# A hybrid encoder kernel in which the 64x64 matmuls change row halves, the sample is padded to 64 tokens and GpSimd makes part of the low weights

## The chip, the cores and the metric

The kernel runs on one core of a Trainium2 chip. The metric is the device time of one execution in microseconds. TensorE (PE) does the matmuls, VectorE (DVE), ScalarE (ACT) and GpSimd (POOL) the elementwise work, and SyncE (SP) issues the transfers.

## What is computed

Two layers of a streaming encoder trunk, for a prompt of 512 tokens and a sample of 32 tokens with states and caches of its own. In each layer (CHUNK = 64, head dimension 64, width 1024):

```
hn = rmsnorm(x);  proj = hn @ w_in          # retention q,k,v,g | GLA q,k,v,g,low | attention q,k,v
retention (4 heads): scores = (q k^T) * decay, intra = scores v, inter = q S * q_decay, S = gamma^L S + (k*k_decay)^T v
GLA (4 heads):  b = cumsum(log_f);  scores[t,s] = sum_d q[t,d] k[s,d] exp(b[t,d]-b[s,d]),  s <= t
                intra = scores v,  inter = (q exp(b)) S,  S = exp(b_last) S + (k exp(b_last-b))^T v
attention (8 heads): own chunk and 8 chunks back, learned relative bias, softmax
x = x + concat[norm(ret)*silu(g), norm(gla)*silu(g), att] @ w_out
x = x + relu(rmsnorm(x) @ w_up)^2 @ w_down
```

## The kernel before

**Units.** All weights are cut into units of 128 columns (1024x128 each, 512 KB). A layer has 28 units of the input projection, 8 of the output projection and 4 groups of 16 for the MLP, 100 in all. SP loads a unit into one of 4 buffers `raw` (`load`, L364), ACT rounds it to fp32r as `whi` (`split`, L487), VectorE takes the remainder `wlo = raw - whi` (`rest`, L762), and TensorE multiplies in three passes (hi by hi, hi by lo, lo by hi) with 544 tokens in two halves of 272 (`products`, L1245): 24 matmuls for a half unit, 48 for a unit. There are two buffers each of `whi` and `wlo`. `rest` of unit n+1 stands in VectorE's queue in unit n, `begin(n)` (L1236) has TensorE wait for it, and `load` has SP wait for it before it reuses the raw buffer.

**Slots.** The mixing of the tokens is cut into stages that are hung by hand into the half units (`PE_STEPS`, `DVE_STEPS`, `ACT_STEPS`). In slot (n, half) TensorE runs the stage and then the 24 products of that half (L1523). The stages in `MID` (L79) stand behind the first 12 products instead. VectorE and ACT have the reading side of the same stages in their queues, each in program order.

**The stages that matter here**, with two groups g of two heads; head p of a group lies in partitions 64p to 64p+63:
- diagonal (L1293), (5,0) for GLA and (11,1) for retention: q by k per chunk and head, 32 matmuls of 64x64 in the order of `chunks()` (p, then g, then chunk c), which read rows 64p and write rows 64 (c mod 2) of PSUM bank M0 + p, and 4 for the sample of 32 columns. VectorE multiplies them by a mask into `Pm` and `Ps` (L928).
- level 0 to 5 (L1309), (5,1) to (8,0): the scores of GLA at block sizes H = 32 to 1. ACT makes factors (`level_f`, L658), VectorE multiplies them into q (`level_q`, L881) and GpSimd into k (`level`, L444), TensorE does 32 matmuls 64x64 by 32 columns and from level 1 on 4 for the sample (64x32 by 16 columns), and VectorE copies the results into `Pm` and `Ps` under a mask (L953). On TensorE a level is done in two pieces: head 0 ahead of the 24 products, head 1 behind the first 12.
- tok (L1332): transposes of k and v; kv (L1350): the states, 32 matmuls in the order c, g, p, with rows 64 (c mod 2) and bank M0 + c mod 2, and 4 for the sample with 32 rows. VectorE runs a chain of 18 state updates (L989).
- out (L1369): 32 matmuls `Pm` by v, with rows and PSUM rows 64 (c mod 2), and 32 matmuls q by S, with rows 64p; out_s (L1387) the same for the sample: 4 of 32x32, 4 of 64x32.
- gn and back (L1405): the norm of the heads on VectorE and ACT, then transposes back; for retention in slot (15, 1), behind 12 products. `newton` (L774) is VectorE's part of the norm.

GpSimd has in a layer two clears, the k products of the levels, eight sums of squares after the output projection with one reduction over the partitions, and 32 additions in the MLP.

The order of the chunks, and what stands between the products:

```
def chunks(head=None):
    for p in range(2) if head is None else (head,):
        for g in range(2):
            for c in range(NC):
                yield p, g, c
...
products(n, (xhi, xlo), all_kc[:4], parts=(half,), last=False)
for st in PE_STEPS.get((n, half), []):
    if st[0] == "level" or st in MID:
        stage(st, 1)
products(n, (xhi, xlo), all_kc[4:], parts=(half,), first=False)
```

Of the kernel before, what the change touches and what calls it, by code (L numbers as in the profile page):

```python
# [20 lines left out]
P = 128  # L21
# [76 lines left out]
for _steps in (DVE_STEPS, ACT_STEPS):  # L98
    for _u in range(4):
        _slot = (15 + 3 * _u, 0)  # L100
        _steps[_slot] = _steps[_slot] + [("parts", _u, 0)]
SLOTS = [(n, half) for n in range(2, N_IN) for half in range(2)]
# [34 lines left out]
def hybrid_encoder(nc, x, wu, w_low, a2, small, wf, bias, bias_s, st_ret, st_gla, ck, cv,  # L137
# [3 lines left out]
    with ctx:  # L141
# [63 lines left out]
        Ps = at("Ps", [TS, 4, TS], o + 14336)  # L205
        S = at("S", [P, 2, NC + 1, HD], o + 14848)
        Ss = at("Ss", [P, 2, 2, HD], o + 19456)
        O = at("O", [P, 20 * HD], o + 20480)
        end1 = o + 25600
# [18 lines left out]
        PS = ctx.enter_context(nc.psum_tensor("PS", [P, 8, 512], F32))  # L228

# [5 lines left out]
        def sem(name):  # L235
# [21 lines left out]
            "pe_back", "back_read", "rot_ready", "ret_scaled", "o_cleared", "s_cleared",  # L257
# [101 lines left out]
        with nc.Fori(0, L) as layer:  # L359
            with nc.Block() as block:  # L360
                @block.sync
                def _(sp):

                    def load(n, j):  # L364
                        if not (isinstance(n, int) and n == RAW):
                            sp.wait_ge(sems["w_lo"], n - RAW)
                        sp.dma_start(raw[j][:, :], wu[layer * UNITS + n, :, :]).then_inc(sems[f"w_in{j}"], 16)
# [65 lines left out]
                def _(pool):  # L433
# [8 lines left out]
                    nc.gpsimd.memset(S[:, :, 0, :], 0.0).then_inc(sems["s_cleared"], 1)  # L442

# [14 lines left out]


# [19 lines left out]
                def _(act):  # L479
# [36 lines left out]
                    def stage(st):  # L516
# [32 lines left out]
                        elif what == "tok":  # L549
# [22 lines left out]
                        elif what == "out_s":  # L572
                            act.wait_ge(sems["o_cleared"], 1)
                            act.wait_ge(sems["pe_out_s"], st[1] + 1)
                            nc.scalar.activation(O[0:TS, 16 * HD:], PS[0:TS, M0, 0:256], ACT.Copy) \
# [11 lines left out]
                        elif what == "back":  # L587
                            kind = st[1]
                            act.wait_ge(sems["pe_back"], kind + 1)
                            for g in range(2):  # L590
                                j = 2 * (1 - kind) + g
                                nc.scalar.activation(oT[j][:, 0:TP], PS[:, M0 + g, :], ACT.Copy)
                                ins = nc.scalar.activation(oT[j][:, TP:T], PS[:, M0 + 2, g * TS:(g + 1) * TS], ACT.Copy)
# [160 lines left out]
                def _(dve):  # L754
# [137 lines left out]
                    def stage(st):  # L892
# [35 lines left out]
                        elif what == "diag":  # L928
# [4 lines left out]
                            dve.wait_ge(sems["pe_diag"], kind + 1)  # L933
                            for p in range(2):
# [5 lines left out]
                                    Ps[:, 2 * p:2 * p + 2, :], PS[0:TS, M0 + 2 + p, 0:2 * TS].rearrange("p (g c) -> p g c", g=2),  # L940
                                    dm_sb[0:TS, kind, 2 * p:2 * p + 2, 0:TS], ALU.mult)
# [11 lines left out]
                        elif what == "level":  # L953
# [17 lines left out]
                            for p in range(2):  # L971
# [5 lines left out]
                                if H <= TS // 2:  # L977
                                    out = Ps[:, 2 * p:2 * p + 2, :].rearrange("p s (b x h) -> p s b x h", x=2, h=H)[:, :, :, 1, :]
                                    m = lm_sb[0:TS, l:l + 1, 0:16].to_broadcast([TS, 2, 16]).rearrange("p s (b h) -> p s b h", h=H)
                                    ins = nc.vector.copy_predicated(out, m, PS[0:TS, M0 + b0 + p, 256:288]  # L980
                                                                    .rearrange("p (s b h) -> p s b h", s=2, h=H))
# [41 lines left out]
                        elif what == "out_s":  # L1023
                            kind = st[1]
                            dve.wait_ge(sems["outs_act"], kind + 1)
                            for p in range(2):
                                o_v = O[0:TS, 16 * HD:].rearrange("p (a b c) -> p a b c", b=2, c=HD)[:, :, p, :]
                                nc.vector.tensor_tensor(o_v, PS[0:TS, M0 + 1 + p, 0:2 * HD].rearrange("p (a c) -> p a c", c=HD),
# [108 lines left out]
                    for n, half in SLOTS:  # L1137
# [3 lines left out]
                        if half == 0 and rest_first:  # L1141
# [5 lines left out]
                        if half == 0 and not rest_first:  # L1147
# [72 lines left out]
                def _(pe):  # L1220
# [45 lines left out]
                    def stage(st, quarter=0):  # L1266
# [26 lines left out]
                        elif what == "diag":  # L1293
# [9 lines left out]
                            for p in range(2):  # L1303
                                for g in range(2):
                                    r, o = slice(64 * p, 64 * p + 64), slice(g * T + TP, (g + 1) * T)
                                    last = mm(PS[0:TS, M0 + 2 + p, g * TS:(g + 1) * TS], k[r, o], q[r, o])
                            last.then_inc(sems["pe_diag"], 1)
                            give((0, 1, 2, 3), "diag_read", kind + 1)
                        elif what == "level":  # L1309

                            l, piece = st[1], quarter % 2
# [11 lines left out]
                            if H <= TS // 2:  # L1323
                                for p in (piece,):
                                    for g in range(2):
                                        r, o = slice(64 * p, 64 * p + 64), slice(g * T + TP, (g + 1) * T)
# [459 lines left out]
```

## Time and profile before

| | us |
|---|---|
| median of 3 runs | 1461.77 (1461.52 to 1462.84) |
| profiled execution, from first to last instruction | 1460.0 |
| PE busy | 1418.2 (97%) |
| DVE busy | 799.6 (55%) |
| ACT busy | 532.5 (36%) |
| POOL busy | 147.8 (10%) |
| mean granted TensorE clock | 0.992 of full |

The page gives no total for the profiled execution other than its span; the runs' times stand 1.8 us above it, for what lies before the first and behind the last instruction. Layer 0 fills the span to about 724 us, layer 1 repeats it from 733 on; every time named below is one of layer 0, and layer 1 has the same 712.7 us later.

### The profile page before, as it was taken

How to read it: one execution, taken by the hardware profiler on the slowest of the kernel's cores; microseconds unless marked ns; L12 is line 12 of the kernel's file. 1: busy time of each engine (PE TensorE's matmuls, PEld its weight loads, DVE VectorE, ACT ScalarE, POOL GpSimd, SP SyncE). 2: the span in 40 equal slices, each digit the busy share in tenths (PEclk: the TensorE clock that was granted, in tenths of full speed). 3: DMA queues.
4: the chain of work that ended last, by engine and by line, in shares of the span. 5: the costliest groups of instructions: out<-in, count | busy, mean ns of one | idle time of the engine just before them, and what ended most of it. 6: DMA issues, size and time to landing. Idle time of an engine off the chain costs nothing. (4 is left out here: it accounts for less than half of the span.)

```text
span 1460.0 us, 30389 instructions
## 1 busy us (share of the span) xinstructions
PE 1418.2 (97%) x12680; PEld 1373.7 (94%) x12680; DVE 799.6 (55%) x1245; ACT 532.5 (36%) x892; POOL 147.8 (10%) x133
## 2 busy tenths in 40 slices
PE   7999999999999999999899999999999999999995
PEld 6999898899999999999889998989999999999995
DVE  4788766744534435344368967776453353443533
ACT  5332465743313223133153226656332231322322
POOL 0110000022020110200202000000201102002012
PEclk9999999999999999999989999999999999999998
DMA  5212343222222222222221133342222222222223
GB/s 193 74 45 65 100 149 93 74 87 88 87 88 86 87 87 88 90 90 89 64 76 48 60 97 106 92 122 73 85 90 87 87 86 86 86 86 87 88 87 107
DMA packets 60683, 129.98 MB, mean 89 GB/s; under 512 B 11984, under 2 KB 29648, under 8 KB 60592
## 3 DMA queue, kind: packets, MB, share of 16 engines
q1 hardware_dynamic: 60592, 128.69, 27.4%
q8 instruction: 66, 1.08, 0.3%
q14 instruction: 25, 0.20, 0.0%
HBM read 121.46 MB, written 7.21 MB: 88 GB/s over the span
## 5 line engine op out<-in xcount | busy, mean ns | idle before, releaser
L1234 PE MATMUL PS<-xhi,whi 128*128 128x272 f32 x1920 | 564.7, 294 | 10.9 <-issue 8.3
L1234 PE MATMUL PS<-xhi,wlo 128*128 128x272 f32 x1920 | 556.7, 290 | 0.0
L1234 PE MATMUL PS<-xlo,whi 128*128 128x272 f32 x1920 | 554.4, 289 | 0.0
L765 DVE TENSOR_TENSOR wlo<-raw,whi 128x1024 fp32r<-128x1024 f32 x200 | 252.7, 1264 | 378.9 <-ACT whi L495 378.2
L495 ACT ACTIVATE whi<-raw 128x1024 fp32r<-128x1024 f32 x200 | 211.6, 1059 | 605.3 <-PE PS L1234 605.0
L1234 PEld LDWEIGHTS PS<-xhi,whi 128*128 128x128 f32 x1920 | 363.3, 189 | 22.2 <-issue 17.8
L1234 PE MATMUL PS<-zhi,wlo 128*128 128x272 f32 x1280 | 370.5, 289 | 0.0
L1234 PE MATMUL PS<-zhi,whi 128*128 128x272 f32 x1280 | 368.4, 288 | 0.4 <-DVE wlo L765 0.4
L1234 PE MATMUL PS<-zlo,whi 128*128 128x272 f32 x1280 | 368.4, 288 | 0.0
L1234 PEld LDWEIGHTS PS<-xlo,whi 128*128 128x128 f32 x1920 | 363.6, 189 | 0.2
L1234 PEld LDWEIGHTS PS<-xhi,wlo 128*128 128x128 f32 x1920 | 362.9, 189 | 0.0
L1234 PEld LDWEIGHTS PS<-zhi,whi 128*128 128x128 f32 x1280 | 240.9, 188 | 0.9 <-DVE wlo L765 0.9
L1234 PEld LDWEIGHTS PS<-zlo,whi 128*128 128x128 f32 x1280 | 241.1, 188 | 0.0
L1234 PEld LDWEIGHTS PS<-zhi,wlo 128*128 128x128 f32 x1280 | 240.8, 188 | 0.0
L475 POOL TENSOR_TENSOR h<-h,sq 128x544 f32<-128x544 f32 x64 | 87.5, 1367 | 664.9 <-DVE sq L1194 664.9
L1186 DVE TENSOR_TENSOR zlo<-nt,zhi 128x544 fp32r<-128x544 f32 x64 | 50.0, 782 | 46.3 <-ACT zhi L693 46.3
L693 ACT ACTIVATE zhi<-nt 128x544 fp32r<-128x544 f32 x64 | 42.1, 658 | 90.4 <-DVE nt L1183 90.4
L1194 DVE TENSOR_TENSOR sq<-PS,r 128x544 f32<-128x544 f32 x64 | 45.9, 717 | 25.9 <-PE PS L1234 25.9
L625 ACT ACTIVATE Pr<-Pr,mx 128x128 f32<-128x128 f32 (+1 forms) x64 | 35.2, 552 | 34.8 <-DVE mx L1080 34.8
L1183 DVE SCALAR_TENSOR_TENSOR nt<-PS,nt 128x544 f32<-128x544 f32 x64 | 45.8, 716 | 0.0
L467 POOL TENSOR_SCALAR ssum<-sq 128x544 f32<-128x544 f32 x2 | 2.4, 1190 | 423.4 <-ACT sq L682 423.4
L690 ACT ACTIVATE nt<-PS 128x544 f32<-128x544 f32 x64 | 38.9, 608 | 0.0
(240 smaller groups left out, 1151.9 us busy)
## 6 DMA issues: line engine op xcount, KB each, us to landing
raw<-in_wu SPq DMA_DIRECT2D x204, 512.0 KB, 3.4
Bh<-in_bias SPq DMA_DIRECT2D x16, 256.0 KB, 3.8
xin<-in_x SPq DMA_DIRECT2D x8, 256.0 KB, 4.3
ckb<-in_ck SPq DMA_DIRECT2D x8, 256.0 KB, 3.7
cvb<-in_cv SPq DMA_DIRECT2D x8, 256.0 KB, 4.3
out_k_p<-ktk SPq DMA_DIRECT2D x8, 256.0 KB, 2.4
out_v_p<-vtk SPq DMA_DIRECT2D x8, 256.0 KB, 2.4
out_y_p<-yt SPq DMA_DIRECT2D x4, 512.0 KB, 2.7
```

The source lines that it names most:

```text
L467: nc.gpsimd.tensor_scalar(ssum[:, :], sq[0][:, :], 1.0, 0.0, ALU.mult, ALU.add) \
L475: nc.gpsimd.tensor_tensor(h[:, m, :], h[:, m, :], sq[m % 2][:, :], ALU.add) \
L495: nc.scalar.activation(whi[n % SPL][:, :], raw[n % RAW][:, :], ACT.Copy).then_inc(sems["w_hi"], 1)
L625: ins = nc.scalar.activation(r, r, ACT.Exp, bias=mx[:, p, i:i + 1], accum_out=rs[:, p, i:i + 1])
L690: nc.scalar.activation(halves(r), PS[:, 2 * (n % 2):2 * (n % 2) + 2, 0:HT], ACT.Relu) \
L693: nc.scalar.activation(zhi[:, k, :], r[:, :], ACT.Copy).then_inc(sems["z_hi"], 1)
L765: nc.vector.tensor_tensor(wlo[n % SPL][:, :], raw[n % RAW][:, :], f32(whi[n % SPL][:, :]), ALU.subtract).then_inc(sems["w_lo"], 1)
L1183: nc.vector.scalar_tensor_tensor(halves(r), PS[:, 2 * (n % 2):2 * (n % 2) + 2, 0:HT], 0.0, halves(r), ALU.max, ALU.mult).then_inc(sems["un ...
L1186: nc.vector.tensor_tensor(zlo[:, k, :], r[:, :], f32(zhi[:, k, :]), ALU.subtract) \
L1194: nc.vector.tensor_tensor(halves(sq[m % 2]), PS[:, 2 * (n % 2):2 * (n % 2) + 2, 0:HT], halves(r2), ALU.mult).then_inc(sems["unit_read"], 1)
L1234: return nc.tensor.matmul(out, lhsT, rhs, start=start, stop=stop, skip_group_check=True)
```

## The change

- `chunks()` goes g, pairs of chunks, p: after two matmuls the head changes, and with it, where rows are 64p, the row half.
- A level is one stage of 32 (+4) matmuls ahead of the 24 products.
- The sample is taken as a window of 64 tokens (the last 32 of the prompt and the 32 of the sample), so that its matmuls are 64x64; its results are read from partitions 32 to 63. GpSimd clears `Ps` and the sample's rows of `ktok` and `vtok` once per layer, and ACT and VectorE wait for that before they write them.
- GpSimd computes `wlo` of units 10 to 20 of each layer; `begin` and `load` wait on a semaphore of its own for these.

```diff
+POOL_UNITS = list(range(10, 21))
+def by_dve(n):
+    return n - sum(m <= n for m in POOL_UNITS)
+def by_pool(n):
+    return sum(m <= n for m in POOL_UNITS)
...
-        Ps = at("Ps", [TS, 4, TS], o + 14336)
+        Ps = at("Ps", [CH, 4, CH], o + 14336)
...
+        def window(g):
+            return slice((g + 1) * T - CH, (g + 1) * T)
...
                     def load(n, j):
-                        if not (isinstance(n, int) and n == RAW):
-                            sp.wait_ge(sems["w_lo"], n - RAW)
+                        if not isinstance(n, int):
+                            sp.wait_ge(sems["w_lo"], n - RAW - len(POOL_UNITS))
+                        elif n - RAW in POOL_UNITS:
+                            sp.wait_ge(sems["w_lo_pool"], by_pool(n - RAW))
+                        elif n > RAW:
+                            sp.wait_ge(sems["w_lo"], by_dve(n - RAW))
...
+                    nc.gpsimd.memset(Ps[:, :, :], 0.0).then_inc(sems["late_cleared"], 1)
+                    nc.gpsimd.memset(ktok[0:CH, NT, :], 0.0).then_inc(sems["late_cleared"], 1)
+                    nc.gpsimd.memset(vtok[0:CH, NT, :], 0.0).then_inc(sems["late_cleared"], 1)
...
                     for l in range(len(LEVELS)):
                         level(l)
+                    for n in POOL_UNITS:
+                        pool.wait_ge(sems["w_hi"], n)
+                        nc.gpsimd.tensor_tensor(wlo[n % SPL][:, :], raw[n % RAW][:, :], f32(whi[n % SPL][:, :]),
+                                                ALU.subtract).then_inc(sems["w_lo_pool"], 1)
...
                             act.wait_ge(sems["pe_tok"], n + 1)
+                            act.wait_ge(sems["late_cleared"], 3)
...
-                            nc.scalar.activation(dst[0:TS, NT, :], PS[0:TS, M0 + 2, 0:256], ACT.Copy) \
+                            nc.scalar.activation(dst[TS:CH, NT, :], PS[TS:CH, M0 + 2, 0:256], ACT.Copy) \
...
                             dve.wait_ge(sems["pe_diag"], kind + 1)
+                            dve.wait_ge(sems["late_cleared"], 3)
...
-                        if half == 0 and rest_first:
+                        if half == 0 and rest_first and n + 1 not in POOL_UNITS:
                             rest(n + 1)
...
-                        if half == 0 and not rest_first:
+                        if half == 0 and not rest_first and n + 1 not in POOL_UNITS:
                             rest(n + 1)
...
                     def begin(n, g=0):
-                        if n:
-                            pe.wait_ge(sems["w_lo"], g * N_MLP + n)
+                        if n in POOL_UNITS:
+                            pe.wait_ge(sems["w_lo_pool"], by_pool(n))
+                        elif n:
+                            pe.wait_ge(sems["w_lo"], g * N_MLP + by_dve(n))
...
-                    def chunks(head=None):
-                        for p in range(2) if head is None else (head,):
-                            for g in range(2):
-                                for c in range(NC):
+                    def chunks():
+                        for g in range(2):
+                            for c in range(0, NC, 2):
+                                for p in range(2):
                                     yield p, g, c
+                                    yield p, g, c + 1
...
-                                    last = mm(PS[0:TS, M0 + 2 + p, g * TS:(g + 1) * TS], k[r, o], q[r, o])
+                                    last = mm(PS[0:CH, M0 + 2 + p, g * CH:(g + 1) * CH], k[r, o], q[r, o])
...
-                            if piece == 0:
-                                take(b0, b0 + 1)
-                                pe.wait_ge(sems["qk_pool"], l + 1)
-                                pe.wait_ge(sems["qk_dve"], l + 1)
-                            for p, g, c in chunks(piece):
+                            take(b0, b0 + 1)
+                            pe.wait_ge(sems["qk_pool"], l + 1)
+                            pe.wait_ge(sems["qk_dve"], l + 1)
+                            for p, g, c in chunks():
...
-                                for p in (piece,):
-                                    for g in range(2):
-                                        r, o = slice(64 * p, 64 * p + 64), slice(g * T + TP, (g + 1) * T)
+                                for g in range(2):
+                                    for p in range(2):
+                                        r, o = slice(64 * p, 64 * p + 64), window(g)
...
-                                    mm(PS[0:TS, M0, (2 * g + p) * HD:(2 * g + p + 1) * HD], Ps[:, 2 * p + g, :],
-                                       vtok[0:TS, NT, f:f + HD])
+                                    mm(PS[0:CH, M0, (2 * g + p) * HD:(2 * g + p + 1) * HD], Ps[:, 2 * p + g, :],
+                                       vtok[0:CH, NT, f:f + HD])
...
                         for st in PE_STEPS.get((n, half), []):
-                            if st[0] == "level" or st in MID:
-                                stage(st, 1)
+                            if st in MID:
+                                stage(st)
```

The transposes of tok and back, kv, the second half of out_s and the reads by ACT and VectorE change in the same way: `0:TS` becomes `0:CH` on TensorE and `TS:CH` for the readers.

## Rows read from the trace of the kernel before

**Rows 1.** The page: the span, and busy time, share, instructions.

```profile
span 1460.0 us, 30389 instructions
...
PE 1418.2 (97%) x12680; PEld 1373.7 (94%) x12680; DVE 799.6 (55%) x1245; ACT 532.5 (36%) x892; POOL 147.8 (10%) x133
```

**Rows 2.** Groups of TensorE by shape: names, count | busy us, mean ns | idle before.

```profile
L1234 PE MATMUL PS<-QK 64*64 64x32 f32 x768 | 26.9, 220 | 2.2 <-DVE Ps L939 2.2
```

**Rows 3.** Timeline of TensorE, units 5 and 6: start us, us, what, count [idle before].

```profile
57.74 2.16 PE L1234 MATMUL PS<-gq,gk 64*64 64x64 f32 x72
...
64.20 1.12 PE L1234 MATMUL PS<-QK 64*64 64x32 f32 x32 [1.08 <-DVE Ps L939]
...
66.74 0.29 PE L1234 MATMUL PS<-xhi,wlo 128*128 128x272 f32 x1
...
68.01 0.39 PE L1234 MATMUL PS<-xhi,whi 128*128 128x272 f32 x1
...
69.49 0.29 PE L1234 MATMUL PS<-xhi,wlo 128*128 128x272 f32 x1
69.70 1.35 PE L1234 MATMUL PS<-QK 64*64 64x32 f32 x36
70.98 0.39 PE L1234 MATMUL PS<-xhi,whi 128*128 128x272 f32 x1
71.21 0.29 PE L1234 MATMUL PS<-xlo,whi 128*128 128x272 f32 x1
```

**Rows 4.** Waits: who waited for whom, us in total, times, longest.

```profile
PE PS L1414 <- DVE O L1046: 2.2, 2, 1.1
```

**Rows 5.** Timeline of TensorE: the kv stage and the two halves of out.

```profile
107.82 1.59 PE L1234 MATMUL PS<-vtok,ktok 64*64 64x64 f32 x72
...
115.56 2.02 PE L1234 MATMUL PS<-vtok,Pm 64*64 64x64 f32 x61
...
117.48 1.86 PE L1234 MATMUL PS<-S,qe_g 64*64 64x64 f32 x63
```

**Rows 6.** Stretches of 0.40 us, L1234: us, PE busy (x records), clock, DMA.

```profile
58.00:58.40 0.40, 0.40 (x22) 1.00 0.00 0
...
108.30:108.70 0.40, 0.40 (x42) 1.00 0.00 0
```

**Rows 7.** Stretches, VectorE alone: us, DVE busy (x instructions), clock, DMA share, GB/s.

```profile
57.93:64.10 6.17, 6.17 (x10) 1.00 0.01 4
81.79:99.34 17.55, 14.56 (x26) 1.00 0.11 33
99.34:114.85 15.51, 15.23 (x33) 1.00 0.22 69
```

**Rows 8.** Timeline of GpSimd: products for levels 0 and 2.

```profile
60.74 0.74 POOL L452 TENSOR_TENSOR QK<-F,gk 128x256 f32<-128x256 f32 x1 [39.63 <-ACT F L666]
...
68.51 1.34 POOL L452 TENSOR_TENSOR QK<-F,gk 128x544 f32<-128x544 f32 x1 [4.66 <-ACT F L666]
```

**Rows 9.** Timeline of GpSimd and of VectorE in the MLP, around 436 us.

```profile
435.97 1.36 POOL L475 TENSOR_TENSOR h<-h,sq 128x544 f32<-128x544 f32 x1 [2.61 <-DVE sq L1194]
...
436.10 2.31 DVE L765 TENSOR_TENSOR wlo<-raw,whi 128x1024 fp32r<-128x1024 f32 x1 [0.21 <-ACT whi L495]
```

**Rows 10.** Timeline of ACT and of VectorE at retention's norm.

```profile
162.91 1.04 ACT L495 ACTIVATE whi<-raw 128x1024 fp32r<-128x1024 f32 x1
...
164.41 0.18 DVE L776 TENSOR_TENSOR gst<-gst 128x20 f32<-128x20 f32 x1 [0.75 <-ACT gst L585]
```

**Rows 11.** Stretches at the layer's end: us, PE busy (x), granted clock, DMA.

```profile
724.00:727.00 3.00, 0.57 (x5) 1.00 0.00 0
727.00:728.00 1.00, 0.00 (x0) 0.82 0.00 0
...
732.00:735.00 3.00, 2.11 (x9) 0.50 0.37 127
735.00:738.00 3.00, 3.00 (x16) 0.52 0.30 74
```

More of the change, by code:

```diff
@@ L574, in stage @@
                             act.wait_ge(sems["pe_out_s"], st[1] + 1)
-                            nc.scalar.activation(O[0:TS, 16 * HD:], PS[0:TS, M0, 0:256], ACT.Copy) \
+                            nc.scalar.activation(O[TS:CH, 16 * HD:], PS[TS:CH, M0, 0:256], ACT.Copy) \
                                 .then_inc(sems["outs_act"], 1)
@@ L592, in stage @@
                                 nc.scalar.activation(oT[j][:, 0:TP], PS[:, M0 + g, :], ACT.Copy)
-                                ins = nc.scalar.activation(oT[j][:, TP:T], PS[:, M0 + 2, g * TS:(g + 1) * TS], ACT.Copy)
+                                ins = nc.scalar.activation(oT[j][:, TP:T], PS[:, M0 + 2, g * CH + TS:(g + 1) * CH], ACT.Copy)
                                 ins.then_inc(sems["back_read"], 1)
@@ L977, in stage @@
                                 if H <= TS // 2:
[L978 to L981, printed above, removed]
+                                    out = Ps[TS:CH, 2 * p:2 * p + 2, TS:CH].rearrange("p s (b x h) -> p s b x h", x=2, h=H)[:, :, :, 1, :]
+                                    m = lm_sb[TS:CH, l:l + 1, 16:32].to_broadcast([TS, 2, 16]).rearrange("p s (b h) -> p s b h", h=H)
+                                    ins = nc.vector.copy_predicated(out, m, PS[TS:CH, M0 + b0 + p, 256:320]
+                                                                    .rearrange("p (s c) -> p s c", s=2)[:, :, 16:32]
+                                                                    .rearrange("p s (b h) -> p s b h", h=H))
                             ins.then_inc(sems["lev_read"], 1)
@@ L1323, in stage @@
                             if H <= TS // 2:
-                                for p in (piece,):
-                                    for g in range(2):
-                                        r, o = slice(64 * p, 64 * p + 64), slice(g * T + TP, (g + 1) * T)
+                                for g in range(2):
+                                    for p in range(2):
+                                        r, o = slice(64 * p, 64 * p + 64), window(g)
                                         rhs = t[r, o].rearrange("p (b x h) -> p b x h", x=2, h=H)[:, :, 1, :]
-                                        last = mm(PS[0:TS, M0 + b0 + p, 256 + 16 * g:272 + 16 * g], t[r, o], rhs)
-                            if piece == 1:
-                                last.then_inc(sems["pe_lev"], 1)
-                                give((b0, b0 + 1), "lev_read", l + 1)
+                                        last = mm(PS[0:CH, M0 + b0 + p, 256 + 32 * g:288 + 32 * g], t[r, o], rhs)
+                            last.then_inc(sems["pe_lev"], 1)
+                            give((b0, b0 + 1), "lev_read", l + 1)
                         elif what == "tok":
@@ L1345, in stage @@
                                                         src[:, g * T + i * P:g * T + (i + 1) * P], ident[:, :])
-                                last = nc.tensor.transpose(PS[0:TS, M0 + 2, g * P:(g + 1) * P],
-                                                           src[:, g * T + TP:(g + 1) * T], ident[:, :])
+                                last = nc.tensor.transpose(PS[0:CH, M0 + 2, g * P:(g + 1) * P], src[:, window(g)], ident[:, :])
                             last.then_inc(sems["pe_tok"], 1)
@@ L1364, in stage @@
                                     last = mm(PS[64 * p:64 * p + 64, M0 + 2, g * HD:(g + 1) * HD],
-                                              ktok[0:TS, NT, f:f + HD], vtok[0:TS, NT, f:f + HD])
+                                              ktok[0:CH, NT, f:f + HD], vtok[0:CH, NT, f:f + HD])
                             last.then_inc(sems["pe_kv"], 1)
@@ L1399, in stage @@
                                     r = slice(64 * p, 64 * p + 64)
-                                    last = mm(PS[0:TS, M0 + 1 + p, g * HD:(g + 1) * HD], qe[r, g * T + TP:(g + 1) * T],
-                                              Ss[r, g, 0, :])
+                                    last = mm(PS[0:CH, M0 + 1 + p, g * HD:(g + 1) * HD], qe[r, window(g)], Ss[r, g, 0, :])
                             last.then_inc(sems["pe_out_s"], 1)
@@ L1415, in stage @@
                                     else:
-                                        last = nc.tensor.transpose(PS[:, M0 + 2, g * TS:(g + 1) * TS], O[0:TS, o:o + P],
-                                                                   ident[0:TS, 0:TS])
+                                        last = nc.tensor.transpose(PS[:, M0 + 2, g * CH:(g + 1) * CH], O[0:CH, o:o + P],
+                                                                   ident[0:CH, 0:CH])
                             last.then_inc(sems["pe_back"], 1)
```

23 lines of the change are left out of this document (12 added, 11 removed).

## The prediction

> **What bounds the kernel now.** The page comes first: TensorE is busy 97% of the 1460.0 us [rows 1]. That share counts pipelined matmuls and does not say whether they run at their best, so next come the groups by shape: behind the products of 128x272, which carry the time, the level stages are the largest, with 768 records of 64x64 [rows 2]. The program has 384 such matmuls (2 layers, 6 levels, 32): each float32 matmul leaves two records. The timeline of TensorE then gives what a stage costs. Between two pieces stand 12 products: from 68.01 to 69.49 are 11 steps, the first of 0.23, so 0.125 each and 3.0 us for a half unit of 24. A level piece stretches one such gap to 1.27 us (66.74 to 68.01) without the sample's matmuls and to 1.49 us (69.49 to 70.98) with them, and the product behind it takes 0.23 instead of 0.125 (70.98 to 71.21) [rows 3]. So a piece costs 1.25 or 1.47 us, a level (two pieces) 2.50 or 2.94 us. TensorE's longest waits for another engine within a layer are at level 0 (1.08 us, on VectorE's reading of the diagonal stage) and in the turn back of retention (1.1 us, once per layer) [rows 3, 4], both on VectorE. TensorE's path plus its waits is the time.
>
> **Do row halves overlap?** The diagonal stage and the kv stage both issue 72 records of nearly the same shapes. Kv, which changes the row half after every four matmuls, takes 1.59 us, the diagonal, which stays in one row half for 16 matmuls, 2.16 us [rows 3, 5]. In 0.40 us the diagonal stage has 22 records under way or started, kv has 42 [rows 6]; as a record lasts 0.22 us, that is some 22 in 0.62 us against 42 in 0.62 us: 64 records in 1.8 or in 0.94 us. With a slower first step I take 0.99 us for the 64 records of a stage whose row halves alternate, 15 ns a start. The Trainium skill speaks against this (TensorE: Matmul & The Clock Gate, section "Wait — 56ns, not 53.3ns?"): starts never come closer than about 25 ns, so that 64 records would need 1.6 us. Kv's rows differ from that rule, and the measurement decides.
>
> **The change on TensorE, per layer.**
> - Levels 1 to 5: one stage instead of two pieces: entry 0.22, 64 records 0.99, the sample's 8 records, now of the same 64x64 mode and on two tiles, 0.23 (four steps of 0.058, the step of kv's rate), exit and slower first product 0.15 + 0.10, less the 0.125 of an ordinary gap: 1.57 against 2.94, five times 1.37 = 6.9. Level 0 has no sample part: 1.34 against 2.50, 1.2. Together 8.1.
> - Two diagonal stages: kv's rate instead of their own, 0.7 each, 1.4. The padded sample part is longer by 0.1 and has no change of mode, 0.
> - Two out stages: two halves of 64 records (the first starts 1.92 before the second, whose 63 records last 1.86 [rows 5]). The half Pm by vtok takes its row half from the chunk, not from the head: it alternates already and has only two tiles in either order, so it gains nothing. The half q by S gains 0.75 each: 1.5.
> - Kv and out_s lose a change of mode each to the padding: 0.1 twice, 0.05 twice, 0.2 in all with rounding.
> - The transposes of the padded sample: same count, weights 64 columns instead of 32: under 0.1, taken as 0.
> That is 11.2 per layer (bounds: 3.1, where 64 records keep 1.85: 0.5 for each of levels 1 to 5, 0.3 for level 0, 0.3 for padding; and 11.5).
>
> **What comes back as a wait, per layer.**
> - Level 0: VectorE is busy without a gap from 57.93 to 64.10 [rows 7], and the wait ends with its last read. The diagonal's 0.7 just lengthens it: -0.7.
> - Levels 3 to 5: the slots shrink, VectorE's work does not. From the end of unit 6 to the reading of level 5 it has 14.56 us of work [rows 7]. TensorE will be at the first transpose behind level 5 after 3 x (1.57 + 3.0) + 0.22, and VectorE starts 0.3 to 0.4 behind the last product: 13.5 to compare. The difference is 1.2 with a hand-over of 0.15, and GpSimd's product for level 4 (1.34) now falls into VectorE's two cosine and sine products, which it blocks (below) for most of its length, 1.1: -2.3 (bounds 0 and 2.9).
> - The state of GLA: from 99.34 to 114.85 VectorE has 15.23 of work [rows 7], less one moved remainder 1.15, plus a block of 2.4: 16.5. TensorE took from 99.34 to the out stage at 115.56 [rows 5] for the same stretch, 16.2, less 0.15 to its first transpose and 0.1 of kv: 16.0: -0.5 (0 and 2.9).
>
> **The remainders on GpSimd.** One takes VectorE about 1.2 us, 1.15 to the next start. GpSimd's products take 0.74 for 256 columns and 1.34 for 544 [rows 8]: by slope 1024 columns take 2.37, by proportion 2.5; I take 2.4. TensorE does not wait for them: ACT makes its half at the start of the unit before, which lasts 6.0 us (two halves) and more, so about 2 us are left; that cover is gone where ACT comes 2 us later. SP's reloads wait for them too; a raw buffer has four units (24 us) to come round. The cost is elsewhere. A VectorE remainder that starts 0.13 after GpSimd's addition lasts 2.31 instead of about 1.2, that is to 1.1 behind GpSimd's end at 437.33 [rows 9]. A VectorE operation with both inputs in SBUF stands still until GpSimd is through. The Trainium skill has the same rule (SBUF — State Buffer, "Who interferes with whom": an exclusive lock for the whole instruction), and the trace agrees. Which operations are behind it? In the attention units the remainders of 17 to 20 would run while VectorE reads PSUM: 0. Unit 16's is the dear one. ACT issues its half at 162.91, just ahead of the logarithm and exponential of retention's norm, so GpSimd starts at 164.0 and holds the port to 166.4; VectorE's first step of the norm, at 164.41, has both inputs in SBUF, and the turn back on TensorE waits for that chain already [rows 4, 10]. -2.0 (0, if it starts behind the chain, and 2.4). Unit 16's own product no longer waits for VectorE: +0.1; a block ahead of tok k of retention: -0.2.
> Nothing for three clears (GpSimd idles 39.6 us before level 0 [rows 8]), the wait on them, and the wider reads of the sample (other partitions, same columns).
>
> **Sum.** 11.2 - 0.7 - 2.3 - 0.5 - 2.0 - 0.1 = 5.6 a layer, 11.2 in all. The profiled span is 1460.0, the median 1461.8, 1.8 more for what lies around it, which is unchanged: 1448.8 and 1450.6.
>
> **Rivals.**
> - The moved remainders cost nothing (the block misses the norm and the state): 8.1 a layer, 1445.6. For: VectorE loses 11 x 1.15 = 12.7 of queue. Against: ACT's order puts unit 16's half right in front of the norm. If levels 3 to 5 were not late either, 1441.
> - The clock. TensorE now stands 1.1 before the turn back and would stand 3.1. At the layer's end it stood from 724.6, the granted clock fell between 727 and 728, and TensorE ran from 732.9 to about 737.9 at 1.2 GHz, which costs 2.4 [rows 11]. The same here twice: 1455.4. A stand of 3.1 us is just as long as that one was when the clock fell; against it, the chain may be shorter by some tenths.
> - Row halves do not overlap in these stages, kv's rate being its own (banks, four matmuls in a row): 3.1 of merging and padding less 2.0: 1459.6, no change. A floor under the distance of two starts would lie between: with 0.25 saved on each of the ten stretches of 64 records that gain, and merging as before, 5.6 less 2.0, 1454.6. The Trainium skill's 25 ns (same page) is such a floor.
> - Slower: the port binds VectorE in units 10 to 20. Eleven blocks of 2.4 replace eleven remainders of 1.15, 13.7 more per layer if each lands on an operation on the path. It decides from 8.1 a layer on; whole, it gives 1473. From 99.3 to 114.9 VectorE has 0.3 us idle [rows 7] to take it up; against it, only two or three of the eleven fall there, and where VectorE reads PSUM nothing is blocked.
>
> **How the numbers follow.** My forecast 0.56, moved remainders free 0.20, clock 0.13, floor 0.02, no overlap 0.05, port 0.04. Changes within 0.2% (2.9 us, about what a measurement of this kernel tells from none) are the no-overlap case: faster 0.91, same 0.05, slower 0.04. The range runs from between 1445.6 and 1441 to the clock case with a block more: 1444 to 1457.5.
>
> **What would show it.** Level stages once per level, 64 or 72 records in about 1.2 to 1.4 us, and 42 records in 0.40 us; out stages near 3.1 us, their first half unchanged. 22 GpSimd remainders of 2.4 us. The wait before level 0 near 1.8, one or two waits around levels 4 and 5, and before the turn back about 3.1, with VectorE's first norm step lasting over 2 us. No such step, and the first rival holds; 1.2 GHz behind it, the second. The prediction is wrong if levels keep 1.8 us for 64 records, or if TensorE waits for a remainder made by GpSimd.

## The result and the profile after

| | before | changed |
|---|---|---|
| median of the runs, us | 1461.91 (1461.52 to 1462.84) | 1469.01 (1467.94 to 1469.95) |
| profiled span, us | 1460.0 | 1467.7 |
| PE busy, us | 1418.2 | 1403.1 |
| mean granted clock | 0.992 | 0.986 |

The ratio is 1.0045, with a 95% interval of 1.0033 to 1.0057: slower, where 1450.6 was forecast. First the page of the changed kernel.

```profile
span 1467.7 us, 30359 instructions
...
PE 1403.1 (96%) x12680; PEld 1361.8 (93%) x12680; DVE 804.8 (55%) x1223; ACT 533.8 (36%) x892; POOL 206.1 (14%) x161
```

TensorE is busy 15 us less than in [rows 1] and the span is 7.7 us longer: the stages did get shorter, and more than that came back as idle time. The group of the level matmuls and two stretches of 0.40 us, one in the diagonal stage and one in a level (from:to and length in us; busy time and records of PE, PEld, DVE, ACT and POOL; granted clock; DMA share; GB/s), say the same.

```profile
L1268 PE MATMUL PS<-QK 64*64 64x32 f32 x848 | 15.9, 220 | 9.2 <-DVE QK L920 5.0 <-DVE Ps L971 4.3
```

```profile
59.20:59.60 0.40, 0.40 (x43) 0.40 (x37) 0.40 (x1) 0.00 (x0) 0.00 (x0) 1.00 0.00 0
71.80:72.20 0.40, 0.40 (x42) 0.40 (x36) 0.40 (x1) 0.40 (x1) 0.00 (x0) 1.00 0.00 0
```

Where [rows 2] had 26.9 us busy and 2.2 idle, there are now 15.9 busy and 9.2 idle; 42 and 43 records in 0.40 us are kv's rate of [rows 6], not the diagonal's 22. Row halves overlap in these stages. The timeline of TensorE in layer 0 shows where the time went instead (start, us, what, count, idle before).

```profile
58.89 1.43 PE L1268 MATMUL PS<-gq,gk 64*64 64x64 f32 x72
...
65.68 1.14 PE L1268 MATMUL PS<-QK 64*64 64x32 f32 x64 [2.14 <-DVE Ps L971]
...
71.47 1.36 PE L1268 MATMUL PS<-QK 64*64 64x32 f32 x72
...
86.12 1.36 PE L1268 MATMUL PS<-QK 64*64 64x32 f32 x72 [1.08 <-DVE QK L920]
...
91.83 1.36 PE L1268 MATMUL PS<-QK 64*64 64x32 f32 x72 [1.15 <-DVE QK L920]
...
98.59 0.63 PE L1379 MATMUL PS<-ident,gv 128*128 128x128 f32 x4 [2.19 <-DVE Ps L1013]
...
115.27 1.99 PE L1268 MATMUL PS<-vtok,Pm 64*64 64x64 f32 x61 [0.26 <-issue]
...
117.15 1.13 PE L1268 MATMUL PS<-S,qe_g 64*64 64x64 f32 x62
...
127.36 1.40 PE L1268 MATMUL PS<-rq,rk 64*64 64x64 f32 x72 [1.76 <-DVE O L1062]
...
168.59 1.43 PE L1447 MATMUL PS<-ident,O 128*128 128x128 f32 x8 [3.25 <-DVE O L1080]
```

The stages are short as forecast (a level in 1.36, the second half of the out stage in 1.13 instead of 1.86), and every wait of over 1 us in these rows is for VectorE. (Waits named below without a row are the distance to the start before them, less the ordinary 0.1 to 0.2.) Three were forecast in kind (level 0; levels 4, 5 and tok; the turn back); the one at retention's diagonal stage was not, nor was one of 0.9 before the turn of the probabilities at 188.45. VectorE's timeline and GpSimd's show what holds VectorE there.

```profile
104.21 2.88 DVE L882 TENSOR_TENSOR rk<-rot,sq 32x544 f32<-32x544 f32 x1
...
122.22 0.72 DVE L881 TENSOR_TENSOR rq<-rot,sq 32x544 f32<-32x544 f32 x1
122.95 2.88 DVE L882 TENSOR_TENSOR rq<-rot,sq 32x544 f32<-32x544 f32 x1
125.86 0.72 DVE L845 TENSOR_TENSOR rv<-PS,rstd 128x544 f32<-128x544 f32 x1
126.62 0.48 DVE L1062 TENSOR_TENSOR O<-PS,O 32x128 f32<-32x128 f32 x2
...
165.08 2.00 DVE L807 TENSOR_TENSOR gst<-gst 128x20 f32<-128x20 f32 x1 [0.75 <-ACT gst L616]
...
183.16 3.40 DVE L1121 TENSOR_SCALAR Pr<-Pr,rs 128x128 f32<-128x128 f32 x4
```

```profile
104.11 2.39 POOL L487 TENSOR_TENSOR wlo<-raw,whi 128x1024 fp32r<-128x1024 f32 x1 [13.02 <-ACT whi L525]
...
122.85 2.39 POOL L487 TENSOR_TENSOR wlo<-raw,whi 128x1024 fp32r<-128x1024 f32 x1 [7.72 <-ACT whi L525]
...
164.70 2.35 POOL L487 TENSOR_TENSOR wlo<-raw,whi 128x1024 fp32r<-128x1024 f32 x1 [10.54 <-ACT whi L525]
```

The same rotary step takes 0.72 free and 2.88 beside a remainder on GpSimd, and it ends 0.6 behind GpSimd. Behind the one at 122.95 in VectorE's queue stands the reading of out_s (L1062), and the diagonal stage waits for its banks. The last wait comes the same way from the remainder of unit 18 at 183.51, which holds the step `Pr` times `rs` (3.40 for four instead of 1.27). That step is a TENSOR_SCALAR. Another one, of 128x20 with a single tensor as input and two constants (L1074, at 134.88), lasted 2.27 beside the remainder of unit 13, where the kernel before had 0.17; TensorE did not wait for it. So operations with two inputs in SBUF are not the only ones that are held.

Last the clock. Stretches of TensorE around 67 and around 130 us:

```profile
63.00:65.50 2.50, 0.54 (x5) 0.32 (x3) 2.46 (x5) 1.19 (x4) 2.01 (x2) 1.00 0.00 0
65.50:67.00 1.50, 1.32 (x66) 1.31 (x67) 1.47 (x3) 0.00 (x0) 0.00 (x0) 1.00 0.05 11
67.00:68.00 1.00, 1.00 (x8) 1.00 (x8) 1.00 (x2) 0.00 (x0) 0.00 (x0) 0.75 0.11 12
68.00:70.00 2.00, 2.00 (x11) 2.00 (x11) 1.45 (x3) 1.20 (x2) 0.01 (x1) 0.50 0.77 244
...
125.00:127.30 2.30, 0.60 (x5) 0.38 (x4) 2.21 (x5) 0.17 (x1) 0.24 (x1) 1.00 0.00 0
127.30:129.00 1.70, 1.64 (x74) 1.60 (x75) 1.09 (x2) 0.25 (x1) 0.00 (x0) 0.98 0.15 34
129.00:130.00 1.00, 1.00 (x6) 1.00 (x5) 0.97 (x3) 0.00 (x0) 0.00 (x0) 0.50 0.69 164
```

In both, behind a wait of some 2 us and one short stage, the granted clock goes to 0.50, that is 1.2 GHz, and the products start 0.227 apart instead of 0.125. It did not fall behind every such wait: in this same trace there was none behind the waits of 2.2 at tok in layer 0 and of 2.1 at level 0 and 1.8 at retention's diagonal in layer 1. Counting the extra 0.1 of each such step: 1.6 behind level 0, 1.6 behind retention's diagonal and 1.3 behind the turn back in layer 0; 1.6 behind tok and 1.3 behind the turn back in layer 1: 7.3 in all, where the kernel before had none within a layer.

**The account of the profiled execution.** Stages shorter: 12.0 a layer, -23.9. Waits longer: 10.8 in layer 0 and 12.0 in layer 1, +22.8. Half clock within the layers +7.3; at the start and at the layer's end, where both kernels have it, 5.2 instead of 4.05, +1.2; the first transfer landed 0.4 later. That makes +7.8 against +7.7. So close an agreement is partly luck: transposes that ran at half clock and the program's end, 0.3 shorter, are not counted apart, and either would move the sum by some tenths.

### The profile page after: what moved, and what is told of

Read it like the earlier page. It is cut to its first block and busy times, and to the rows that moved or that the text cites. A ratio compares the mean times of both kernels' runs of the same rounds, so it can differ in the third digit from the quotient of the medians.

```text
span 1467.7 us, 30359 instructions
## 1 busy us (share of the span) xinstructions
PE 1403.1 (96%) x12680; PEld 1361.8 (93%) x12680; DVE 804.8 (55%) x1223; ACT 533.8 (36%) x892; POOL 206.1 (14%) x161
## 3 DMA queue, kind: packets, MB, share of 16 engines
q1 hardware_dynamic: 60592, 128.69, 26.9%
## 5 line engine op out<-in xcount | busy, mean ns | idle before, releaser
L796 DVE TENSOR_TENSOR wlo<-raw,whi 128x1024 fp32r<-128x1024 f32 x178 | 225.1, 1265 | 378.1 <-ACT whi L525 377.7
L1268 PEld LDWEIGHTS PS<-xlo,whi 128*128 128x128 f32 x1920 | 367.3, 191 | 0.2
L1268 PEld LDWEIGHTS PS<-xhi,wlo 128*128 128x128 f32 x1920 | 366.6, 191 | 0.0
L487 POOL TENSOR_TENSOR wlo<-raw,whi 128x1024 fp32r<-128x1024 f32 x22 | 53.1, 2412 | 178.5 <-ACT whi L525 178.5
L478 POOL TENSOR_TENSOR QK<-F,gk 128x544 f32<-128x544 f32 (+1 forms) x14 | 23.0, 1654 | 117.1 <-ACT F L697 117.1
```

What stands on the lines that cost most here:

```text
L478: ins = nc.gpsimd.tensor_tensor(q[:, :, 0, :], f[:, :, 0, :], k[:, :, 0, :], ALU.mult)
L487: nc.gpsimd.tensor_tensor(wlo[n % SPL][:, :], raw[n % RAW][:, :], f32(whi[n % SPL][:, :]), ALU.subtract).then_inc(sems["w_lo_pool"], 1)
L796: nc.vector.tensor_tensor(wlo[n % SPL][:, :], raw[n % RAW][:, :], f32(whi[n % SPL][:, :]), ALU.subtract).then_inc(sems["w_lo"], 1)
L1268: return nc.tensor.matmul(out, lhsT, rhs, start=start, stop=stop, skip_group_check=True)
```

## The experiments

Three parts can be made apart: the order (with the level as one stage), the padding, GpSimd's remainders. The first five runs, with the two kernels, are all their combinations but one (padding with GpSimd). Times below are medians beside runs of the kernel before on the same chip (1462.98, 1462.92 and 1463.31 in the three sets); where two kernels of different sets are compared, each is taken by its distance to the kernel before, which for the changed kernel is +7.1.

**No remainders on GpSimd.**

```diff
-POOL_UNITS = list(range(10, 21))
+POOL_UNITS = []
```

> The changed kernel, but VectorE makes all low weights again. Theory A (the remainders on GpSimd are the larger part of the loss): the three blocked steps go (rq 2.88 us, norm step 2.00, Pr times rs 2.53), with them the waits before the diagonal of retention (1.8), in front of the turn back (the 2.15 more than before) and before the turn of probabilities (0.9), and the 3.4 us stretches at half clock behind them, 1.7 us each, two per layer: about 8.2 a layer, 16 in all, so 1452 to 1455 and faster than both kernels. The half-clock stretches behind level 0 or tok stay. Theory B (the clock falls because the level stages are now denser and the waits around them longer, and GpSimd only fills idle VectorE time): at most the 2.2 in front of the turn back returns, 1463 to 1466.

1457.28, ratio 0.996 (0.9946 to 0.9973): 5.7 faster than before, so the remainders cost 12.8 (7.1 and 5.7) of the changed kernel's time. The wait of 1.8 at retention's diagonal fell to 0.25, the one of 0.9 is gone, and the one before the turn back fell from 3.25 to 1.6; one wait that came in their place is due to VectorE's longer queue (tok k of retention, 1.2), which is part of why it is 12.8 and not 16.

```profile
PE PS L1268 <- DVE QK L920: 4.5, 4, 1.2
PE PS L1379 <- DVE Ps L1013: 4.4, 2, 2.2
PE PS L1268 <- DVE Ps L971: 4.3, 2, 2.1
PE PS L1447 <- DVE O L1080: 3.2, 4, 1.4
...
PE PS L1379 <- DVE rk L984: 2.2, 2, 1.1
```

Half-clock steps within the layers fell from 7.3 to 4.4: one behind level 0, one behind the turn back, one in layer 1. Theory A stands in its mechanism; the time is 2.3 beyond its range, with 12.8 gained of the 16 expected.

**GpSimd's remainders alone**, in the kernel before (its own order, pieces and sample; `POOL_UNITS` and the waits of `begin` and `load` as in the change).

> The kernel before, with only the low weights of units 10 to 20 moved to GpSimd. Theory A: the same three waits appear without any change of the matmuls, with half-clock stretches behind the longer ones: 10 to 16 us slower than before, 1472 to 1478. Theory B: the wait before the turn back grows by 2 a layer and nothing else, 1466.

1479.38, ratio 1.0108 (1.0092 to 1.0123): 16.4 slower. The same steps are held, with no change of any matmul:

```profile
123.78 0.72 DVE L877 TENSOR_TENSOR rq<-rot,sq 32x544 f32<-32x544 f32 x1
124.52 2.87 DVE L878 TENSOR_TENSOR rq<-rot,sq 32x544 f32<-32x544 f32 x1
```

```profile
PE PS L1441 <- DVE O L1073: 6.0, 3, 2.9
...
PE PS L1261 <- DVE O L1055: 3.2, 2, 1.6
```

Waits of 1.7 at retention's diagonal, 3.0 before the turn back (1.1 before) and 0.9 before the turn of the probabilities, and 6.5 us of half-clock steps behind the first two. The mechanism is theory A's; the time is 1.4 beyond its range of 1472 to 1478.

**The changed kernel without padding** (windows, clears and readers of the sample back to `TS` rows from partition 0).

```diff
-            return slice((g + 1) * T - CH, (g + 1) * T)
+            return slice(g * T + TP, (g + 1) * T)
```

> The changed kernel with the sample of 32 tokens as before (partitions 0 to 31), so VectorE's reads of the sample overlap their neighbours again. By the traces the padded reads cost VectorE 0.37 us per level and 0.36 per diagonal stage; levels 1 to 5 are 1.5 us of the 4.7 us that TensorE waits at levels 4, 5 and tok, and 0.36 of the wait at level 0. TensorE pays about 0.1 per stage for the change of mode, 1.0 a layer. Theory A': waits at levels 4, 5 and tok fall from 4.7 to about 3.2, level 0 from 2.2 to 1.9, net gain 0.8 a layer, 1467.4, or up to 3.4 a layer more if a half-clock stretch goes with them. Rival (the padded reads are not what lengthens VectorE's queue): waits unchanged, 1470 to 1471.

1460.85, ratio 0.9986 (0.9977 to 0.9995): 9.2 gained against the changed kernel, where I had expected about 1.6 and at most 8.4. The waits at levels 4, 5 and tok fell from 4.6 to 2.8 and level 0 by 0.3, and half-clock steps from 7.3 to 3.5. The direction was right, the size was not: my 1.6 counted no clock at all, and the 3.8 us less of half-clock steps is two fifths of the gain.

**Padding alone**, in the kernel before.

> The kernel before with the padded sample alone (order of chunks, pieces of a level and VectorE's low weights as before). VectorE's level reads get 0.37 us longer each but VectorE has 0.9 to 1.6 us idle before them, so only the wait at level 0 grows by 0.36; TensorE saves the changes of mode, 0.6 to 1.0 a layer: 1460.5 to 1461.5, no change within 0.2%. If the longer VectorE reads bind in the levels even there: 1463 to 1465.

1467.70, ratio 1.0043 (1.003 to 1.0057), with runs from 1464.8 to 1472.6: the main expectation missed, and the median lies above the rival's range (1463 to 1465) too. In its profiled execution (1464.77, the fastest of the five) there are waits of 0.35 more at level 0, 0.5 at tok v, 0.3 at tok k of retention and 0.3 before the turn back, and one half-clock stretch of 1.3 behind level 0 in layer 1. VectorE's longer reads bind even where it had idle time. What the slower executions lose besides, up to 8 us, no trace shows; so the 4.7 is less sure than the other differences.

**The order alone.** No padding, no remainders on GpSimd.

> Only the order of the chunks and the level as one stage: the sample as before, VectorE makes all low weights. If the effects found so far add (GpSimd part worth 11.7 against the changed kernel, padding 8.2): 1449.0, faster than before by 13 and the best so far. If the two share a loss (the longer VectorE queue behind the levels): 1451 to 1453. Waits of about 2.1, 0.9, 1.1 and 1.4 remain at levels 0, 4, 5 and tok, since the moved remainders have no part in them.

1448.47, ratio 0.9898 (0.9883 to 0.9913): 14.5 faster, as expected if the parts add (1449.0). The sum of the three parts alone, -14.5 + 16.4 + 4.7 = +6.6, is near the +7.1 of the whole, but not because the parts are independent: padding costs 4.7 alone and 8.7 beside the new order, the remainders 16.4 alone and 12.3 beside it. The two deviations happen to cancel. No half-clock step within a layer in this trace.

```profile
83.44 1.37 PE L1261 MATMUL PS<-QK 64*64 64x32 f32 x72 [0.67 <-DVE QK L916]
...
88.84 1.37 PE L1261 MATMUL PS<-QK 64*64 64x32 f32 x72 [0.84 <-DVE QK L916]
...
94.48 0.63 PE L1372 MATMUL PS<-ident,gv 128*128 128x128 f32 x4 [1.05 <-DVE Ps L1007]
```

**A level in two pieces again**, by group instead of by head, so that heads still alternate.

```diff
-                            for p, g, c in chunks():
+                            for p, g, c in chunks(piece):
```

> As the run with the order alone, but each level in two pieces of 16 (+2) matmuls, one per group of heads, the second behind 12 products as before; heads alternate in both. TensorE pays a second entry and exit per level, about 0.5 us, 2.9 a layer. Theory C (from level 3 on VectorE's queue, lengthened by GpSimd's products for levels 2 and 3, sets the pace): the waits at levels 4, 5 and tok, 2.8 together, take most of it up, so only 0.5 to 1.5 us a layer are lost: 1 to 3 us slower than the order alone. Rival (TensorE's path sets it): the whole 2.9 a layer, 5.8 slower.

1451.51: 3.0 slower than the order alone. In the trace two pieces of a level cost 1.93 against 1.49 for the single stage (level 0: 0.3 more), so TensorE pays 5.1, not the 5.8 expected, and 3.0 of it shows. The waits at levels 4, 5 and tok are 0.2, 0.5 and 0.7 instead of 0.7, 0.9 and 1.1: they took up the rest. Theory C, at its upper end; this trace also has 0.8 of half-clock steps behind level 0.

**Seven of the eleven remainders on GpSimd**, the order otherwise alone.

```diff
-POOL_UNITS = list(range(10, 21))
+POOL_UNITS = [11, 13, 14, 15, 17, 19, 20]
```

> As the run with the order alone, and GpSimd makes the low weights of units 11, 13, 14, 15, 17, 19 and 20 only, whose blocks fell on no VectorE step that TensorE waited for; those of 10, 12, 16 and 18, which blocked the rotary products, the norm and the probabilities, stay on VectorE. Theory A (a remainder on GpSimd costs by what it blocks): no wait at the diagonal of retention above 0.3, the back wait stays near 1.2 to 1.5 and the wait of 1.2 at tok k of retention that VectorE's queue gives in the kernel without GpSimd goes: 1 to 3 us faster than the order alone, 1446 to 1448. Rival (any of them costs, or they land elsewhere once the queue moves): 1450 or more.

1449.13 (1448.3 to 1449.25) against 1448.47 (1446.81 to 1449.06): not told apart, so the hoped gain is a miss. The wait at tok k did shrink (0.83 to 0.40, start to start) and no wait was added; but this trace has half-clock stretches behind level 0 in both layers, 3.2 together, behind the very same wait of 1.9 after which the order alone had none.

**VectorE reads the padded sample from partition 0.** As the kernel without remainders on GpSimd, but `Ps` is read and written on 64 partitions; the upper 32 rows it adds meet rows of `vtok` that are zero.

```diff
-                                    Ps[TS:CH, 2 * p:2 * p + 2, TS:CH],
+                                    Ps[0:CH, 2 * p:2 * p + 2, TS:CH],
```

> As the changed kernel without GpSimd's remainders (1457.3), but VectorE reads and writes the padded sample on partitions 0 to 63 instead of 32 to 63. If it is the start at partition 32 that keeps these small steps from overlapping their neighbours, the level reads take 0.97 us again instead of 1.34 and the kernel gets 2 to 8 us faster, 1450 to 1455. If it is any change of the partitions between neighbours, they stay at 1.34 and the time at 1457.

1450.36 instead of 1457.28, inside the 1450 to 1455 expected if the start at partition 32 is the cause. The other explanation, any change of partitions between neighbours, falls: these reads still change from 128 partitions to 64. The reads of one level on VectorE, first in the changed kernel, then here:

```profile
79.72 0.45 DVE L1008 COPY_PREDICATED Pm<-lm_sb,PS 128x256 f32<-128x256 uint32 x1
80.18 0.19 DVE L1013 COPY_PREDICATED Ps<-lm_sb,PS 32x32 f32<-32x32 uint32 x1
80.38 0.45 DVE L1008 COPY_PREDICATED Pm<-lm_sb,PS 128x256 f32<-128x256 uint32 x1
80.84 0.18 DVE L1013 COPY_PREDICATED Ps<-lm_sb,PS 32x32 f32<-32x32 uint32 x1
```

```profile
72.51 0.45 DVE L1008 COPY_PREDICATED Pm<-lm_sb,PS 128x256 f32<-128x256 uint32 x1
72.84 0.18 DVE L1013 COPY_PREDICATED Ps<-lm_sb,PS 64x32 f32<-64x32 uint32 x1
72.94 0.44 DVE L1008 COPY_PREDICATED Pm<-lm_sb,PS 128x256 f32<-128x256 uint32 x1
73.28 0.18 DVE L1013 COPY_PREDICATED Ps<-lm_sb,PS 64x32 f32<-64x32 uint32 x1
```

The durations are the same; the starts are not: 1.12 from the first to the fourth against 0.77. An operation that starts on partition 32 waits until its forerunner has ended, and so does the one behind it. The Trainium skill states this rule (VectorE: DVE Perf Modes, section "Two Vector instructions with no wait between them"): an instruction is held until every earlier one is finished if one of its inputs starts in another group of 32 partitions than the first input from that memory of the last instruction that read it, or its output in another group than the last output into that memory. The two traces agree.

**Level 0 behind 12 products**, the order otherwise alone.

```diff
-MID = [("back", GLA), ("back", RET), ("turn", 3, 1)]
+MID = [("back", GLA), ("back", RET), ("turn", 3, 1), ("level", 0)]
```

> As the run with the order alone, with level 0 hung behind the first 12 products of its half unit. TensorE then has 1.5 us of work where it waited 1.9 for VectorE's reading of the diagonal stage. Theory (the wait at level 0 is VectorE's queue alone, and VectorE has 2 us idle behind level 0's reading): 1.5 less per layer and no half-clock stretch behind level 0: 1445 to 1446, and less spread between runs. Rival (the level's products come later and the wait moves to level 1 or 2): 1448.

1449.15, no gain, and the theory (1445 to 1446) falls. The rival had the passing on right but not the place, which it put at level 1 or 2: the wait fell to 0.32 at level 0 and stands at level 4, 2.18 instead of 0.67:

```profile
63.89 1.13 PE L1261 MATMUL PS<-QK 64*64 64x32 f32 x64 [0.32 <-DVE Ps L966]
...
82.42 1.37 PE L1261 MATMUL PS<-QK 64*64 64x32 f32 x72 [2.18 <-DVE QK L916]
```

Nor did the clock stay up: the trace has 1.15 and 0.9 of half-clock steps behind the turns back, whose wait is 1.1 as in the kernel before.

**Levels 4 and 5 and the transpose behind 12 products as well** (`("level", 4), ("level", 5), ("tok", GLA, "v")` added to `MID`).

> As the last, and levels 4 and 5 and the first transpose behind them also stand behind the first 12 products. They waited 0.75, 0.9 and 1.15 for VectorE, whose queue is the same: TensorE gets 1.5 us once to catch up with it, so 1.5 of the 2.8 go in each layer, if nothing behind them (kv, out) is late: 1442 to 1443. Rival (VectorE's queue sets the pace through to the out stage of GLA): 1445.

1448.21 (1447.5 to 1448.56): not told apart from the last (1448.18 to 1449.52) or from the order alone, and above both numbers expected. The trace shows why: the wait is passed on again, 0.4 at the out stage, 0.45 at out_s and 0.3 at tok k of GLA, and twice a layer TensorE now stands some 0.3 for a remainder that VectorE makes (at 86.53 and 106.39), which it did not do before. This is the rival's mechanism: VectorE's queue sets the pace from level 0 through to the out stage.

**The same with seven remainders on GpSimd.**

> As the last, with the low weights of units 11, 13, 14, 15, 17, 19 and 20 made by GpSimd. With level 0 moved there is no half-clock stretch left that hides the effect: the wait of 0.7 at tok k of retention falls to 0.3, 0.4 a layer, so 0.5 to 1 us faster than without; if a remainder lands on a VectorE step on the path it is 0 to 2 us slower.

1446.15, ratio 0.9881 (0.9864 to 0.9899): 2.1 faster than the last, where 0.5 to 1 was expected, with ranges that do not meet (1445.66 to 1446.28). It is the best kernel of this study, 17 us below the kernel before. VectorE's busy time is 791.8 instead of the 803.7 of the order alone, the waits at out_s and at retention's diagonal are gone, and that at tok k is 0.25.

**The same with padding**, VectorE on partitions 0 to 63 throughout (units 10 to 20 on VectorE).

> As the run with levels 0, 4, 5 and the transpose behind 12 products, with the padded sample, all of VectorE's reads of it on partitions 0 to 63. If padding costs nothing but the partition-32 starts, only TensorE's saved changes of mode remain: 0.1 for each of some 9 stages, 1 us a layer at most, 1 to 2 us faster than unpadded where TensorE and not VectorE sets the pace. If not, the same time or up to 1 slower.

1447.37 (1446.48 to 1448.79) against 1448.21 (1447.5 to 1448.56) unpadded: less than the 1 to 2 expected, and the ranges overlap. Without the starts on partition 32 the padding neither costs nor brings anything that this measurement shows.

## Why the prediction was wrong

Split by the three parts, the forecast of -11.2 was -15.8 for the order, -0.6 for the padding and +5.2 for the remainders. Measured, each beside those before it, they are -14.5, +8.7 and +12.8, which is +7.0. The order was right; the padding was missed by 9.3 and the remainders by 7.6. The lower clock is a part of both: the profiled execution with the order alone has no half-clock step within a layer, the one with padding as well 4.4 us of them, the changed kernel 7.3.

- **TensorE's part was right.** 11.2 a layer was forecast, 12.0 came: a level costs 1.49 (forecast 1.57), level 0 1.28 (1.34), the diagonals gain 0.73 (0.7), out 0.77 (0.75), with its first half, `Pm` by v, unchanged at 1.9. The rivals without overlap and with a floor under the starts are out. By the 25 ns of the Trainium skill (TensorE: Matmul & The Clock Gate, "Wait — 56ns, not 53.3ns?") 64 records need 1.6, an estimate; level 0's 64 last 1.14 with 0.22 for the last of them, so they start within 0.92. The rule does not hold here.
- **Failed step one: "Nothing for ... the wider reads of the sample (other partitions, same columns)".** The bracket names the difference and prices it at zero. From the first start to the last end it costs VectorE 0.37 at each of levels 1 to 3, 0.5 at levels 4 and 5 and 0.32 per diagonal, on the queue that this same prediction had called the tightest. Measured: 4.7 alone, 8.7 beside the new order, 9.2 beside the order and the remainders. The reads from partition 0 give 6.9 of the 8.7 back. Level 0's wait, 0.35 over the forecast of 1.8, is this too.
- **Failed step two: the places where a remainder meets VectorE.** The mechanism, the 2.4 us and the dear place were right: the norm step lasted 2.00 and the turn back waited 2.15 more (forecast 2.0; 0.3 of it stays without the remainders, so it is the padding's). But the text looked for further places only in units 17 to 20, found PSUM reads and wrote 0, and its condition, both inputs in SBUF, was too narrow. Unit 18's meets `Pr` times `rs` (0.9 a layer), and unit 12's, not looked at, meets the rotary product ahead of the out_s reading (1.8 a layer). Forecast 2.6 a layer, 5.2; measured 16.4 alone and 12.8 in the changed kernel.
- **Failed step three: the clock, which the sum put at nothing.** It was a rival with one place a layer at 2.4. It came behind five waits, 7.3 in the profiled execution, of which the turn back's, the one place named, are 2.6. The price per drop was too high, the number of places too low: waits of some 2 us, with a short stage behind them, were enough in three of six places, and only the one of 3.1 had been looked at.
- **Levels 3 to 5.** Forecast 2.3 a layer; 2.8 without padding, 4.6 with it. The block at level 4 is as priced (the sine product takes 2.00 instead of 0.72). Missed was a second one: GpSimd's product for level 3 now holds VectorE's factor product for 1.15 (1.86 instead of 0.71); in the kernel before it met the weights and cost 0.34.
- The state of GLA waited 0.3 in layer 0 and not at all in layer 1 (forecast 0.5). Taken together, the order alone was forecast at 10.9 less 0.7 less 2.3, 7.9 a layer or 15.8, and brought 14.5. The rival on the other side, the port binding VectorE in units 10 to 20, had the right sign and mechanism at a chance of 0.04; of the eleven remainders five held a VectorE step for over 1 us, three of them one that TensorE waited for. That the time came nearer to its 1473 than to my forecast is partly luck: the padding, which is no part of that rival, made 8.7 of the 21.5 that the order's gain was up against.

What stays open: why the same wait, of 1.9 at level 0 or of some 2 in the changed kernel, is followed by a half-clock stretch in some places and not in others. No run was made to settle it, so how much of a time is the clock's can be read from a trace but could not be forecast.

## What to carry over

Before work is moved to GpSimd, list for each moved instruction which VectorE operation that reads no PSUM can start beside it and who waits behind that one in the queue. Here TENSOR_TENSOR with two SBUF inputs and TENSOR_SCALAR with one were held, and one of 128x20 as long as a large one. A change that gives TensorE time back is worth only what the other queue can follow: moving a stage within the half unit moved the wait, not the end. And where operands move to other partitions, a "same columns, same cost" has to be checked in the distance of starts, not in the durations.

## What was unexpected

- One tensor as input does not save an operation from being held, but the kind of operation matters. In the kernel without padding a remainder runs on GpSimd from 129.40 to 131.87. A reduction passes beside it at its usual 0.41; the TENSOR_SCALAR behind it, 0.17 when free, ends with GpSimd.

```profile
129.40 2.47 POOL L484 TENSOR_TENSOR wlo<-raw,whi 128x1024 fp32r<-128x1024 f32 x1 [7.83 <-ACT whi L522]
```

```profile
130.16 0.41 DVE L883 TENSOR_REDUCE gst<-osq 128x4 f32<-128x256 f32 x1
130.60 1.31 DVE L1067 TENSOR_SCALAR gst<-gst 128x20 f32<-128x20 f32 x1
```

- VectorE operations whose start partition changes between neighbours lose their overlap, about 0.1 at each change, while their own durations hardly change (0.18 and 0.19).
- The half-clock time at the start of the program varied from 1.4 to 2.8 us between the profiled executions of these kernels and at the layer's end from 1.5 to 2.9, with no difference in the work there; so 1 or 2 us between two spans need no other cause.
- A half-clock stretch followed the turn back's wait of 1.4 in the kernel without GpSimd's remainders, and even one of 1.1 in two others (level 0 behind 12 products, and the padded last one), while in the kernel before and most others the 1.1 was followed by none.
